# Gate products of an RG-LRU on the two row halves of the TensorE array

## The chip, the core and the metric

The kernel runs on one core of a Trainium2 chip. The metric is the device time of one execution in microseconds. A core has five engines with queues of their own: TensorE (PE, with its weight loads shown as PEld), VectorE (DVE), ScalarE (ACT), GpSimd (POOL) and SyncE (SP, which issues the DMAs here). Each engine works through its instructions in the order in which they are written, and engines wait for each other on semaphores. Matrix products are written to PSUM, eight banks of 512 float32 in each of 128 partitions; ACT and DVE read them from there.

## The reference

One layer of a hybrid decoder trunk, for a prompt of 2048 rows and for 8 decode sequences of 4 rows. After a normalised and modulated input `hn`, one projection gives six parts. Group A is an RG-LRU: a causal convolution of width 4 gives `xc`, two gates are computed from it, each with a block-diagonal matrix of 8 blocks of 64x64, and a recurrence runs along the rows:

```
r = sigmoid(einsum('blnc,ncd->blnd', xb, wa) + ba)     # xb: xc in 8 blocks of 64
i = sigmoid(einsum('blnc,ncd->blnd', xb, wx) + bx)
log_a = -8 * softplus(-lam) * r
a = exp(log_a);  u = sqrt(max(-expm1(2 * log_a), 0)) * (i * xc)
h[t] = a[t] * h[t-1] + u[t];  ya = h * silu(ga)
```

Group B (HGRN2, four heads of 128) is a chunked recurrence with decays. Both groups are joined, multiplied by an output matrix, normalised and added to the input. All inputs and outputs are float32.

## The kernel before

The prompt is worked in 8 passes (`body(n, ...)`) of 256 rows, the decode rows come after the last. Pass 0 and pass 7 are written out, passes 1 to 6 are a loop. Large products are split into three 16-bit products (`split3`, L390). The products of the recurrences, the gates and the transposes are float32; each float32 product stands in the trace as two records with a weight load each.

The order of all work is written out by hand, engine by engine. In a pass, PE runs the projections of the pass, mixed with eight levels of the HGRN2 recurrence for each half of the heads (`level`, L462 to L469), with the output product of the pass before (`out_rows`), and with the transposes of the next pass's input (`turn_x`). The channels of group A come in two halves, p = 0 and p = 1. For each half there is one call of `gates(n, p)` on PE (L507) and one of `gates_out(n, p)` on ACT (L903, L908), so there are 16 calls of each in the prompt.

The stationary of the gates, `wg`, is 128x128 for each gate and pair of blocks: two 64x64 blocks on its diagonal and zeros elsewhere, which POOL writes at the start (L1661). A call of `gates` makes four products: two of the r gate into one PSUM bank, two of the i gate into the other, each 128 rows by 128 columns by 256 moving columns. The r products raise `gr_ps`, the i products `gi_ps`. The banks are `aux[0]` and `aux[1]`, which the transposes share, so each of the two parts waits for its own bank: in the second call of a pass the r part for the copies of the transposed input (`hn_lo`), the i part for ACT's copy of the transposed keys (`kt_sb`, L865). `gates_out` then makes four sigmoids of 128x256 (two for r, two for i), and raises `r_sig` and `i_sig`.

The first call comes between level 3 and level 4 of the second half of the heads; 24 projection records follow, and then level 4, which needs DVE's scaling of that level's keys (L1166). The second call comes near the end of a pass. After it PE makes `unit(n, 1, 0)`, the rest of an output product, and `unit(n, 1, 1)`; then the next pass begins: it waits for `i_sig` of the second call, makes the 48 records of the projection `FR`, and then `turn_y` (L441), the transposes of the normalised HGRN2 rows. `turn_y` waits for `yb_ok`, that is, for the last instruction of `rows(n, 1)` on DVE (L1195).

What stands on ACT around the second call, in its order:

```
k_out(n, 1); squares_m(n - 1, 2); gates_out(n, 1); squares_o(n, 2)
squares_m(n - 1, 3); squares_o(n, 3); decay(n, 1); root(n, 1)
```

`squares_o` (L872) takes the squares of the HGRN2 rows with a sum, `squares_m` (L861) those of the output product, each activation followed by a read of the accumulator. `rows(n, 1)` on DVE begins when `squares_o(n, 3)` is done: 12 small steps for a reciprocal root, then four multiplications (L1195). After the first call ACT goes on with `xa_out(n, 1)` (L879), which waits for the 24 projection records that follow the gates, then with `decay`, `root` and the copies of the next input (`hn_out`).

In pass 0 the engines also split the weights: ACT copies pieces of the output matrix (L951), and POOL then takes the rests (L1627).

The decode rows have gates of their own: eight products with 32 moving columns (L794) and eight sigmoids (L1081).

Of the kernel before, what the change touches and what calls it, by code (L numbers as in the profile page):

```python
# [38 lines left out]
ACT = mybir.ActivationFunctionType  # L39

P = 128
# [3 lines left out]
CT = DA // P  # L45
# [14 lines left out]
DLEVELS = 2  # L60
NEWTON = 12
MAGIC = float(0x5F3759DF)

# [12 lines left out]
def build(nc, x_prompt, x_sample, state_rglru_h, state_rglru_conv, state_hgrn_S, c_prompt, c_sample, ada_w, ada_b,  # L76
          pre_norm_w, post_norm_w, w_in, conv_w, conv_b, rg_wa, rg_ba, rg_wx, rg_bx, rg_lambda, hg_lb_logits,
          hg_onorm_w, w_out, y_prompt, y_sample, h_prompt, conv_prompt, S_prompt, h_sample, conv_sample, S_sample):
    with ExitStack() as ctx:
# [33 lines left out]
        sil = sb("sil", [P, CT, T])  # L113
        wg = sb("wg", [P, 2, CT, P])

# [57 lines left out]
        u_ps = Signal("u_ps", 4)  # L173
        gr_ps, gi_ps = Signal("gr_ps", 2), Signal("gi_ps", 2)

# [116 lines left out]
        def _(sp):  # L292
# [15 lines left out]
            for i, (kind, c) in enumerate(pieces):  # L308
# [14 lines left out]
                if i == 6:  # L323
                    sp.wait_ge(zeroed, 1)
                    for w, src in ((0, rg_wa), (1, rg_wx)):
                        for odd in range(2):
                            v = src[0].rearrange("(t two) c d -> two c t d", two=2)[odd]
                            sp.dma_start(wg[64 * odd:64 * odd + 64, w, :, 64 * odd:64 * odd + 64], v).then_inc(wg_ld, 16)

# [51 lines left out]
        def _(pe):  # L381
# [50 lines left out]
            def turn_y(n, j):  # L432

                if j == 0:
                    pe.wait_ge(yb_ok.sem, yb_ok.at(n, 8))
                    pe.wait_ge(r_sig.sem, r_sig.at(n, 4))
                else:
                    pe.wait_ge(i_sig.sem, i_sig.at(n, 4))
                for h in range(2):
                    for t in range(NT):  # L440
                        last = nc.tensor.transpose(aux[j][:, T * h + P * t:T * h + P * t + P],  # L441
                                                   gbs[:, t, P * (2 * j + h):P * (2 * j + h) + P], ident[:, :])
                last.then_inc(yt_ps.sem, 1)
# [52 lines left out]
            def gates(n, p):  # L496
                pe.wait_ge(cvc.sem, cvc.at(n, 8 * p + 8))
                for w, s in ((0, gr_ps), (1, gi_ps)):
                    if p == 0 and w == 0:
                        if not isinstance(n, int) or n > 0:  # L500
                            pe.wait_ge(ytl.sem, ytl.at(n - 1, 2))
                    elif w == 1:
                        pe.wait_ge(kt_sb.sem, kt_sb.at(n, p + 1))
                    elif not (isinstance(n, int) and n == BODIES - 1):
                        pe.wait_ge(hn_lo.sem, hn_lo.at(n + 1, 2))
                    for c in range(2):
                        last = mm(aux[(1 + w + p) % 2][:, T * c:T * c + T], wg[:, w, 2 * p + c, :], xc[:, c, :],  # L507
                                  start=True, stop=True)
                    last.then_inc(s.sem, 1)

# [35 lines left out]
            def body(n, first, last_body):  # L546
# [118 lines left out]
                level(n, 1, 6)  # L665
                pe.wait_ge(r_sig.sem, r_sig.at(n, 2))
                if not last_body:
                    turn_x(n + 1, 0)
                    pe.wait_ge(i_sig.sem, i_sig.at(n, 2))
                    turn_x(n + 1, 1)  # L670
# [4 lines left out]
                else:  # L675
                    pe.wait_ge(i_sig.sem, i_sig.at(n, 2))
                    turn_decode()
# [43 lines left out]
            pe.wait_ge(wg_ld, 64)  # L721
            pe.wait_ge(zeroed, 3)
            pe.wait_ge(carry_zero, 2)
# [66 lines left out]
            pe.wait_ge(dv("conv_d"), 16)  # L790
            for w in range(2):
                for c in range(CT):
                    o = TD * CT * w + TD * c
                    last = mm(lev[1][:, o:o + TD], wg[:, w, c, :], xcd[:, TD * c:TD * c + TD], start=True, stop=True)  # L794
            last.then_inc(dv("gates_ps"), 1)
# [47 lines left out]
        def _(act):  # L843
# [54 lines left out]
            def gates_out(n, p):  # L898

                act.wait_ge(gr_ps.sem, gr_ps.at(n, p + 1))  # L900
                act.wait_ge(iu.sem, iu.at(n, p))
                for c in range(2):
                    A(rr[:, c, :], aux[(1 + p) % 2][:, T * c:T * c + T], ACT.Sigmoid,  # L903
                      bias=pcol("ba", 2 * p + c)).then_inc(r_sig.sem, 1)
                act.wait_ge(gi_ps.sem, gi_ps.at(n, p + 1))
                act.wait_ge(scan.sem, scan.at(n, 2 * p))
                for c in range(2):
                    A(ii[:, c, :], aux[p][:, T * c:T * c + T], ACT.Sigmoid, bias=pcol("bx", 2 * p + c)).then_inc(i_sig.sem, 1)  # L908

# [168 lines left out]
            for w, dst, bias in ((0, rrd, "ba"), (1, iid, "bx")):  # L1078
                for c in range(CT):
                    o = W4 * w + TD * c  # L1080
                    A(dst[:, TD * c:TD * c + TD], lev[1][:, o:o + TD], ACT.Sigmoid, bias=pcol(bias, c)).then_inc(dv("ri_d"), 1)  # L1081
            act.wait_ge(dv("ri_d"), 2 * CT)
# [28 lines left out]
        def _(dve):  # L1111
# [325 lines left out]
            rest(2)  # L1437
            dve.wait_ge(zeroed, 3)

# [132 lines left out]
        def _(pool):  # L1572
# [79 lines left out]
            def link(ins):  # L1652
# [7 lines left out]
                            base=0, channel_multiplier=1).then_inc(ident_ok, 1)  # L1660
            G.memset(wg[:, :, :, :], 0.0).then_inc(zeroed, 1)  # L1661
            pool.wait_ge(ident_ok, 1)
# [65 lines left out]
```

## Time and profile before

| what | before |
|---|---|
| median of 3 runs | 1023.69 us (1023.05 to 1025.93) |
| span of the profiled execution | 1026.3 us |
| mean granted TensorE clock | 0.981 |
| PE busy, PEld busy | 984.2 us, 714.3 us |
| DVE busy, ACT busy, POOL busy | 582.0 us, 430.0 us, 161.0 us |

The span runs from the first to the last instruction of one profiled execution, the only time that the page gives of it; it lies 2.6 us above the median of the runs and 0.4 us above the slowest of them. Busy times are sums of the records; matmuls are pipelined, so their records overlap. A granted clock of 1.0 is 2.4 GHz.

### The profile page before, as it was taken

The page shows a single profiled execution, that of the slowest core. Times are in us where ns is not written, and L with a number is a line of the kernel's source. Part 1 is how long each engine was busy: PE and PEld are TensorE (multiplying, and loading weights), DVE is VectorE, ACT ScalarE, POOL GpSimd, SP SyncE. Part 2 cuts the span into 40 slices and gives each one's busy share as a digit, 9 for nine tenths or more (in the row PEclk, how much of TensorE's full clock was granted, in tenths as well). Part 3 has the DMA queues.
Part 4 walks back from the last instruction along what each step waited for, and adds up shares of the span by engine and source line. Part 5 has one row for each costly group of instructions (what it writes and reads, how often), then busy time and mean ns, then how long its engine had stood idle before and what let it go on. Part 6 is the DMA issues. An engine that isn't in the chain of part 4 may idle for free.

```text
span 1026.3 us, 19994 instructions
## 1 busy us (share of the span) xinstructions
PE 984.2 (96%) x7423; PEld 714.3 (70%) x7478; DVE 582.0 (57%) x1652; ACT 430.0 (42%) x810; POOL 161.0 (16%) x208
## 2 busy tenths in 40 slices
PE   7899986899999999999999999999999999999987
PEld 3465875469775887579766976697759775887554
DVE  1453688436763576436754566366635773477445
ACT  2531747313651365135713373237413661345321
POOL 4000024301130112011110112011301130111212
PEclk9999998899999999999999999999999999999998
DMA  9984301100110011000110011001101010100413
GB/s 313 326 275 130 118 24 59 62 2 21 42 63 0 20 41 43 19 20 0 42 62 0 21 41 62 0 21 41 62 0 41 0 50 1 42 1 23 118 42 111
DMA packets 46590, 60.62 MB, mean 59 GB/s; under 512 B 2748, under 2 KB 40208, under 8 KB 46524
## 3 DMA queue, kind: packets, MB, share of 16 engines
q1 hardware_dynamic: 46524, 59.86, 17.8%
q8 instruction: 27, 0.44, 0.2%
q14 instruction: 39, 0.32, 0.1%
HBM read 48.90 MB, written 10.95 MB: 58 GB/s over the span
## 4 chain that ended last, share of the span: by engine, by line
PE 90%; DVE 5%; issue 2%; ACT 1%; DMA 1%; SPq 1%; DVEq 0%; ACTq 0%
PE ring L390 66%; PE lev L464 7%; PE aux L507 3%; PE okv L521 2%; PE lev L469 1%; PE okv L491 1%; PE lev L462 1%; PE ring L521 1%; PE okv L493 1%; PE okv L492 1%; DMA work<-in_w_in_dram 1%; PE okv L811 1%; PE aux L441 1%; PE aux L477 1%; PE aux L428 1%
## 5 line engine op out<-in xcount | busy, mean ns | idle before, releaser
L390 PE MATMUL ring<-hnh,wih 128*128 128x256 bf16 (+1 forms) x1152 | 291.1, 264 | 5.8 <-DVE hnl L1273 4.2
L390 PE MATMUL ring<-hnh,wil 128*128 128x256 bf16 (+1 forms) x1152 | 291.2, 264 | 0.0
L390 PE MATMUL ring<-hnl,wih 128*128 128x256 f16 (+1 forms) x1152 | 291.1, 264 | 0.0
L390 PE MATMUL ring<-woh,work 128*128 128x512 f16 x512 | 162.3, 379 | 1.7
L390 PEld LDWEIGHTS ring<-hnh,wih 128*128 128x128 f16 x1152 | 112.5, 100 | 18.1 <-issue 4.5
L1165 DVE TENSOR_TENSOR qq<-qq,gg 128x256 f32<-128x256 f32 x96 | 44.1, 459 | 140.1 <-PE lev L464 99.8
L390 PEld LDWEIGHTS ring<-hnl,wih 128*128 128x128 f16 x1152 | 110.6, 98 | 12.9
L390 PEld LDWEIGHTS ring<-hnh,wil 128*128 128x128 bf16 x1152 | 110.6, 98 | 12.4
L390 PE MATMUL ring<-wih,hnh 128*128 128x512 f16 (+1 forms) x264 | 101.1, 383 | 4.0 <-ACT kk L851 4.0
L390 PE MATMUL ring<-wih,hnl 128*128 128x512 f16 (+1 forms) x264 | 101.1, 383 | 1.4 <-issue 0.2
L1587 POOL TENSOR_TENSOR kk<-kk,cols 128x256 f32<-128x256 f32 x32 | 29.3, 935 | 419.3 <-ACT kk L851 419.3
L390 PE MATMUL ring<-wil,hnh 128*128 128x512 bf16 (+1 forms) x240 | 91.7, 382 | 0.0
L390 PEld LDWEIGHTS ring<-woh,work 128*128 128x128 bf16 (+1 forms) x512 | 50.2, 98 | 54.8
L464 PEld LDWEIGHTS lev<-qq,kk 128*128 128x128 f32 x640 | 80.9, 192 | 8.5 <-issue 2.3
L390 PE MATMUL ring<-wol,work 128*128 128x512 bf16 x225 | 85.3, 379 | 0.0
L464 PE MATMUL lev<-qq,kk 128*128 128x64 f32 x640 | 80.4, 268 | 1.8 <-DVE kk L1166 1.7
L1183 DVE SCALAR_TENSOR_TENSOR st<-st,gg,okv 128x128 f32<-128x128 f32 x64 | 19.4, 345 | 70.9 <-PE okv L493 70.9
L1173 DVE COPY_PREDICATED am<-lmask,lev 128x256 f32<-128x256 uint8 (+1 forms) x112 | 57.3, 511 | 0.0
L861 ACT ACTIVATE ring<-ring 128x512 f32<-128x512 f32 x32 | 18.6, 582 | 84.0 <-DVE work L1204 84.0
L1607 POOL TENSOR_TENSOR ii<-ii,xc 128x512 f32<-128x512 f32 x16 | 22.9, 1429 | 188.3 <-ACT ii L908 188.2
L390 PEld LDWEIGHTS ring<-wih,hnh 128*128 128x128 bf16 (+1 forms) x264 | 28.2, 107 | 29.6 <-ACT kk L851 4.3
L390 PEld LDWEIGHTS ring<-wih,hnl 128*128 128x128 f16 (+1 forms) x264 | 26.0, 99 | 31.8 <-issue 1.1
(310 smaller groups left out, 1585.5 us busy)
## 6 DMA issues: line engine op xcount, KB each, us to landing
xin<-in_x_prompt_dram SPq DMA_DIRECT2D x16, 512.0 KB, 3.4
work<-in_x_prompt_dram SPq DMA_DIRECT2D x16, 512.0 KB, 4.3
out_dram<-work SPq DMA_DIRECT2D x16, 512.0 KB, 2.6
work<-in_ada_w_dram SPq DMA_DIRECT2D x4, 1024.0 KB, 10.4
woh<-in_ada_w_dram SPq DMA_DIRECT2D x4, 1024.0 KB, 11.8
work<-in_w_in_dram SPq DMA_DIRECT2D x4, 1024.0 KB, 7.2
woh<-in_w_in_dram SPq DMA_DIRECT2D x4, 1024.0 KB, 8.5
wol<-in_w_in_dram SPq DMA_DIRECT2D x4, 1024.0 KB, 9.6
```

The costliest lines, as they stand in the source:

```text
L390: last = mm(out, a(k), b(k), start=start and k == ks[0] and j == 0, stop=stop and k == ks[-1] and j == 2)
L428: last = nc.tensor.transpose(bank[:, (k % 2) * T + P * t:(k % 2) * T + P * t + P], xin[:, t, P * k:P * k + P], ident[:, :])
L441: last = nc.tensor.transpose(aux[j][:, T * h + P * t:T * h + P * t + P], gbs[:, t, P * (2 * j + h):P * (2 * j + h) + P], ident[:, :])
L464: last = mm(lev[i % 2][:, P // 2 * hc:P // 2 * hc + P // 2], k, blocks(q, m)[:, :, 1, :], start=True, stop=True)
L507: last = mm(aux[(1 + w + p) % 2][:, T * c:T * c + T], wg[:, w, 2 * p + c, :], xc[:, c, :], start=True, stop=True)
L521: last = mm(bank[0:NS, o:o + 256], siluc[:, k, :], w[:, k, :], start=k == 0, stop=k == KT - 1)
L861: A(ring[j % 2][:, :], ring[j % 2][:, :], ACT.Square, accum_out=essq[:, j:j + 1]).then_inc(esq[j % 2].sem, 1)
L1165: V.tensor_tensor(qo, qo, g[:, :, 0:1].to_broadcast([P, nb, m]), ALU.mult).then_inc(q_upd.sem, 1)
L1173: V.copy_predicated(a[:, :, :, 1, :], msk, x).then_inc(amask.sem, 1)
L1183: V.scalar_tensor_tensor(st[:, hd, :], st[:, hd, :], gg[:, o:o + 1], okv[c][:, 2 * P + P * h:3 * P + P * h], ALU.mult, ALU.add).then_inc(s ...
L1587: G.tensor_tensor(kk[:, cols], kk[:, cols], omlb[:, hd:hd + 1].to_broadcast([P, T]), ALU.mult)\
L1607: G.tensor_tensor(ii[:, :, :], ii[:, :, :], xc[:, :, :], ALU.mult).then_inc(ix_ok.sem, 1)
```

## The change

Both gates of a pair of blocks share one stationary. `wg` shrinks from 2x4 to 4 tiles of 128x128. In rows 0 to 63 of a tile the r block stands in columns 0 to 63 and the i block in columns 64 to 127; in rows 64 to 127 it is the other way round. A product takes 64 rows of the stationary and 64 rows of `xc`, and gives r and i of one block in the two partition halves of a bank. The product of the even block goes to `aux[0]`, that of the odd block to `aux[1]`, so a call of `gates` still has four products of 256 moving columns, now of 64 rows each. All four are behind one set of waits and raise one semaphore, `g_ps`.

ACT makes each sigmoid on 64 partitions: eight instead of four for each call. The r halves lie in the partitions where they are needed; the i halves are read from one partition half and written to the other. The waits of PE on `r_sig` become waits on `i_sig`. The zero fill of `wg` on POOL goes, and with it SP's wait for it. The decode gates change in the same way: eight products of 64 rows into two banks, sixteen sigmoids.

```diff
-        wg = sb("wg", [P, 2, CT, P])
+        wg = sb("wg", [P, CT, P])
...
-                    sp.wait_ge(zeroed, 1)
                     for w, src in ((0, rg_wa), (1, rg_wx)):
                         for odd in range(2):
                             v = src[0].rearrange("(t two) c d -> two c t d", two=2)[odd]
-                            sp.dma_start(wg[64 * odd:64 * odd + 64, w, :, 64 * odd:64 * odd + 64], v).then_inc(wg_ld, 16)
+                            col = HALF * (w ^ odd)
+                            sp.dma_start(wg[HALF * odd:HALF * odd + HALF, :, col:col + HALF], v).then_inc(wg_ld, 16)
...
             def gates(n, p):
                 pe.wait_ge(cvc.sem, cvc.at(n, 8 * p + 8))
-                for w, s in ((0, gr_ps), (1, gi_ps)):
-                    if p == 0 and w == 0:
-                        if not isinstance(n, int) or n > 0:
-                            pe.wait_ge(ytl.sem, ytl.at(n - 1, 2))
-                    elif w == 1:
-                        pe.wait_ge(kt_sb.sem, kt_sb.at(n, p + 1))
-                    elif not (isinstance(n, int) and n == BODIES - 1):
-                        pe.wait_ge(hn_lo.sem, hn_lo.at(n + 1, 2))
-                    for c in range(2):
-                        last = mm(aux[(1 + w + p) % 2][:, T * c:T * c + T], wg[:, w, 2 * p + c, :], xc[:, c, :],
-                                  start=True, stop=True)
-                    last.then_inc(s.sem, 1)
+                if p == 0:
+                    if not isinstance(n, int) or n > 0:
+                        pe.wait_ge(ytl.sem, ytl.at(n - 1, 2))
+                elif not (isinstance(n, int) and n == BODIES - 1):
+                    pe.wait_ge(hn_lo.sem, hn_lo.at(n + 1, 2))
+                pe.wait_ge(kt_sb.sem, kt_sb.at(n, p + 1))
+                for c in range(2):
+                    for odd in range(2):
+                        k = slice(HALF * odd, HALF * odd + HALF)
+                        last = mm(aux[odd][:, T * c:T * c + T], wg[k, 2 * p + c, :], xc[k, c, :], start=True, stop=True)
+                last.then_inc(g_ps.sem, 1)
...
-                act.wait_ge(gr_ps.sem, gr_ps.at(n, p + 1))
+                act.wait_ge(g_ps.sem, g_ps.at(n, p + 1))
                 act.wait_ge(iu.sem, iu.at(n, p))
                 for c in range(2):
-                    A(rr[:, c, :], aux[(1 + p) % 2][:, T * c:T * c + T], ACT.Sigmoid,
-                      bias=pcol("ba", 2 * p + c)).then_inc(r_sig.sem, 1)
-                act.wait_ge(gi_ps.sem, gi_ps.at(n, p + 1))
+                    for odd in range(2):
+                        k, src = slice(HALF * odd, HALF * odd + HALF), aux[odd][:, T * c:T * c + T]
+                        ins = A(rr[k, c, :], src[k, :], ACT.Sigmoid, bias=pcol("ba", 2 * p + c)[k, :])
+                    ins.then_inc(r_sig.sem, 1)
                 act.wait_ge(scan.sem, scan.at(n, 2 * p))
                 for c in range(2):
-                    A(ii[:, c, :], aux[p][:, T * c:T * c + T], ACT.Sigmoid, bias=pcol("bx", 2 * p + c)).then_inc(i_sig.sem, 1)
+                    for odd in range(2):
+                        k, o = slice(HALF * odd, HALF * odd + HALF), slice(HALF * (1 - odd), HALF * (1 - odd) + HALF)
+                        ins = A(ii[k, c, :], aux[odd][o, T * c:T * c + T], ACT.Sigmoid, bias=pcol("bx", 2 * p + c)[k, :])
+                    ins.then_inc(i_sig.sem, 1)
...
-            G.memset(wg[:, :, :, :], 0.0).then_inc(zeroed, 1)
```

## Rows read from the trace of the kernel before

**Rows 1.** The page: busy time, share of the span and instructions of each engine.

```profile
PE 984.2 (96%) x7423; PEld 714.3 (70%) x7478; DVE 582.0 (57%) x1652; ACT 430.0 (42%) x810; POOL 161.0 (16%) x208
```

**Rows 2.** The page: shares of the chain that ended last, by engine.

```profile
PE 90%; DVE 5%; issue 2%; ACT 1%; DMA 1%; SPq 1%; DVEq 0%; ACTq 0%
```

**Rows 3.** Busy times in one pass: stretch, its length, each engine's time, granted clock.

```profile
394.40:502.80 108.40, 108.03 (x811) 80.72 (x818) 62.17 (x184) 46.63 (x92) 15.22 (x19) 1.00 0.08 29
```

**Rows 4.** Timeline of PE, pass 3, from the second gate call.

```profile
497.19 1.89 PE L507 MATMUL aux<-xc,wg 128*128 128x256 f32 x8
...
502.88 0.27 PE L390 MATMUL ring<-hnh,wih 128*128 128x256 bf16 x1
...
508.18 0.33 PE L441 MATMUL aux<-ident,gbs 128*128 128x128 f32 x1
```

**Rows 5.** Timeline of DVE, pass 3: the rows that `turn_y` waits for.

```profile
506.99 1.13 DVE L1195 SCALAR_TENSOR_TENSOR gbs<-okv,stat,gbs 128x128 f32<-128x128 f32 x4
```

**Rows 6.** Timeline of PE, pass 3, first gate call: start, duration, instructions.

```profile
473.38 1.95 PE L507 MATMUL aux<-xc,wg 128*128 128x256 f32 x8
475.16 0.27 PE L390 MATMUL ring<-hnh,wih 128*128 128x256 bf16 x1
```

**Rows 7.** Timeline of PE: products on parts of the array (rows*columns) and neighbours.

```profile
484.59 0.27 PE L390 MATMUL ring<-hnh,wil 128*128 128x256 bf16 x1
484.79 0.45 PE L469 MATMUL lev<-qq,kk 128*32 128x32 f32 x16
485.17 0.33 PE L428 MATMUL aux<-ident,xin 128*128 128x128 f32 x1
...
958.71 0.41 PE L748 MATMUL lev<-qq,kk 128*32 128x32 f32 x8
```

**Rows 8.** L469 by source: duration ns min/median/max, first and last start, forms.

```profile
L469 PE MATMUL lev<-qq,kk x384: 190/196/270, 83.3 to 923.2; 128*32 128x32 f32 x128, 128*64 128x64 f32 x64
```

**Rows 9.** Timeline of DVE, pass 3, after the first gate call.

```profile
476.20 0.42 DVE L1166 TENSOR_TENSOR kk<-kk,gg 128x256 f32<-128x256 f32 x1
```

**Rows 10.** Timeline of ACT, pass 3, around the second gate call.

```profile
496.09 0.60 ACT L865 ACTIVATE ktr<-aux 128x512 f32<-128x512 f32 x1 [2.76 <-PE aux L477]
...
499.60 0.84 ACT L903 ACTIVATE rr<-aux,par 128x256 f32<-128x256 f32 x2
500.33 0.84 ACT L908 ACTIVATE ii<-aux,par 128x256 f32<-128x256 f32 x2
501.25 0.28 ACT L872 ACTIVATE junk<-okv 128x128 bf16<-128x128 f32 x1
...
502.53 0.58 ACT L861 ACTIVATE ring<-ring 128x512 f32<-128x512 f32 x1 [0.52 <-DVE work L1204]
...
503.81 0.28 ACT L872 ACTIVATE junk<-okv 128x128 bf16<-128x128 f32 x1 [0.59 <-DVE st L1183]
```

**Rows 11.** Groups of ACT by form: count, busy us, mean ns, idle before.

```profile
L941 ACT ACTIVATE rr<-ring 9x512 f32<-9x512 f32 x1 | 0.6, 587 | 5.6 <-PE ring L521 5.6
```

**Rows 12.** Timeline of ACT, pass 3, after the first gate call.

```profile
474.50 0.84 ACT L903 ACTIVATE rr<-aux,par 128x256 f32<-128x256 f32 x2 [3.32 <-PE aux L507]
...
478.12 0.60 ACT L879 ACTIVATE xa<-ring 128x512 f32<-128x512 f32 x1 [1.92 <-PE ring L390]
```

**Rows 13.** Timeline of ACT: a square, its accumulator read, the next activation.

```profile
447.71 0.28 ACT L872 ACTIVATE junk<-okv 128x128 bf16<-128x128 f32 x1
447.88 0.19 ACT L872 ACTIVATION_READ_ACCUMULATOR junk<-okv 128x1 f32 x1
447.98 0.62 ACT L895 ACTIVATE junk<-xin 128x512 bf16<-128x512 f32 x1
```

**Rows 14.** Timeline of PE: the gate products of the decode rows.

```profile
970.34 1.97 PE L794 MATMUL lev<-xin,wg 128*128 128x32 f32 x16
```

**Rows 15.** Timelines of POOL and DVE in pass 0.

```profile
146.82 4.07 POOL L1627 TENSOR_TENSOR wol<-work,woh 128x2048 bf16<-128x2048 f32 x1
...
147.40 3.77 DVE L1165 TENSOR_TENSOR qq<-qq,gg 128x256 f32<-128x256 f32 x1 [2.25 <-PE lev L464]
```

More of the change, by code:

```diff
@@ L61 @@
 NEWTON = 12
+HALF = P // 2
 MAGIC = float(0x5F3759DF)
@@ L173, in build @@
         u_ps = Signal("u_ps", 4)
-        gr_ps, gi_ps = Signal("gr_ps", 2), Signal("gi_ps", 2)
+        g_ps = Signal("g_ps", 2)
         f_sig, k_sig, q_sb = Signal("f_sig", 2), Signal("k_sig", 2), Signal("q_sb", 2)
@@ L435, in turn_y @@
                     pe.wait_ge(yb_ok.sem, yb_ok.at(n, 8))
-                    pe.wait_ge(r_sig.sem, r_sig.at(n, 4))
-                else:
                     pe.wait_ge(i_sig.sem, i_sig.at(n, 4))
@@ L665, in body @@
                 level(n, 1, 6)
-                pe.wait_ge(r_sig.sem, r_sig.at(n, 2))
+                pe.wait_ge(i_sig.sem, i_sig.at(n, 2))
                 if not last_body:
                     turn_x(n + 1, 0)
-                    pe.wait_ge(i_sig.sem, i_sig.at(n, 2))
                     turn_x(n + 1, 1)
@@ L675, in body @@
                 else:
-                    pe.wait_ge(i_sig.sem, i_sig.at(n, 2))
                     turn_decode()
@@ L721, in _ @@
             pe.wait_ge(wg_ld, 64)
-            pe.wait_ge(zeroed, 3)
+            pe.wait_ge(zeroed, 2)
             pe.wait_ge(carry_zero, 2)
@@ L790, in _ @@
             pe.wait_ge(dv("conv_d"), 16)
[L791 to L794, printed above, removed]
+            for c in range(CT):
+                for odd in range(2):
+                    k = slice(HALF * odd, HALF * odd + HALF)
+                    last = mm((lev[1], aux[0])[odd][:, TD * c:TD * c + TD], wg[k, c, :], xcd[k, TD * c:TD * c + TD],
+                              start=True, stop=True)
             last.then_inc(dv("gates_ps"), 1)
@@ L898, in gates_out @@
             def gates_out(n, p):
-                act.wait_ge(gr_ps.sem, gr_ps.at(n, p + 1))
+                act.wait_ge(g_ps.sem, g_ps.at(n, p + 1))
                 act.wait_ge(iu.sem, iu.at(n, p))
                 for c in range(2):
-                    A(rr[:, c, :], aux[(1 + p) % 2][:, T * c:T * c + T], ACT.Sigmoid,
-                      bias=pcol("ba", 2 * p + c)).then_inc(r_sig.sem, 1)
-                act.wait_ge(gi_ps.sem, gi_ps.at(n, p + 1))
+                    for odd in range(2):
+                        k, src = slice(HALF * odd, HALF * odd + HALF), aux[odd][:, T * c:T * c + T]
+                        ins = A(rr[k, c, :], src[k, :], ACT.Sigmoid, bias=pcol("ba", 2 * p + c)[k, :])
+                    ins.then_inc(r_sig.sem, 1)
                 act.wait_ge(scan.sem, scan.at(n, 2 * p))
                 for c in range(2):
-                    A(ii[:, c, :], aux[p][:, T * c:T * c + T], ACT.Sigmoid, bias=pcol("bx", 2 * p + c)).then_inc(i_sig.sem, 1)
+                    for odd in range(2):
+                        k, o = slice(HALF * odd, HALF * odd + HALF), slice(HALF * (1 - odd), HALF * (1 - odd) + HALF)
+                        ins = A(ii[k, c, :], aux[odd][o, T * c:T * c + T], ACT.Sigmoid, bias=pcol("bx", 2 * p + c)[k, :])
+                    ins.then_inc(i_sig.sem, 1)
             def decay(n, p):
@@ L1079, in _ @@
                 for c in range(CT):
-                    o = W4 * w + TD * c
-                    A(dst[:, TD * c:TD * c + TD], lev[1][:, o:o + TD], ACT.Sigmoid, bias=pcol(bias, c)).then_inc(dv("ri_d"), 1)
+                    cols = slice(TD * c, TD * c + TD)
+                    for odd in range(2):
+                        k, o = slice(HALF * odd, HALF * odd + HALF), HALF * (odd ^ w)
+                        ins = A(dst[k, cols], (lev[1], aux[0])[odd][o:o + HALF, cols], ACT.Sigmoid, bias=pcol(bias, c)[k, :])
+                    ins.then_inc(dv("ri_d"), 1)
             act.wait_ge(dv("ri_d"), 2 * CT)
@@ L1437, in _ @@
             rest(2)
-            dve.wait_ge(zeroed, 3)
+            dve.wait_ge(zeroed, 2)
             body(0, True, False)
```

## The prediction

> **What bounds the kernel now.** I read the page's busy times first: PE is busy for 96% of the span, DVE for 57%, ACT for 42% [rows 1]. The chain of waits, second, says the same in another way: 90% of what ended last is PE's own work, 5% DVE's, 1% ACT's [rows 2]. A busy share is an average, so third I cut out one pass of the loop: in 108.40 us PE is busy for 108.03 at the full granted clock (2.4 GHz), ACT for 46.63 and DVE for 62.17 [rows 3]. So in a steady pass a microsecond less of PE work is a microsecond less of time, as long as nobody else is about to be late. Who is about to be late, I looked for in the timeline at the two gate calls, fourth, and there is one place: `turn_y` starts at 508.18, and the DVE instructions that it waits for end at 506.99 + 1.13 = 508.12 [rows 4, 5], while PE's 48 projection records before it end at about the same moment (502.88 to 508.18 is 5.30 us, 0.110 for each) [rows 4]. PE and a chain through ACT and DVE tie there. This stands alike in six passes (1 to 6); in pass 0 and pass 7 it is otherwise, and they are reckoned apart.
>
> **The products.** A call of `gates` makes eight records, and the next product starts 1.78 us after the first: 0.22 for each [rows 6]. After the change there are again eight records, each with the same 256 columns, so the same 0.22, since the step is that of the columns and not of the rows. Nothing is won unless the two halves run beside each other. No row shows two row halves, but the nearest shows two column parts. Level 6 puts 16 records of 128x32 in alternate column parts and takes 0.45 us; the decode's eight records of the same shape, all in one part, take 0.41 [rows 7]. A record lasts 0.196 [rows 8], so the steps are (0.45 - 0.20)/15 = 0.017 and (0.41 - 0.20)/7 = 0.030: two parts go at nearly twice the rate. Parts also have a price. Level 6 starts 0.20 behind the record before it, where 0.11 is usual: 0.09 to get in. It hands over at 485.17, which is 0.38 after its start, and 16 steps are 0.27: some 0.10 to get out [rows 7]. I add 0.10 for filling the second half (between 0 and one step of 0.22). A call then takes 4 x 0.22 + 0.09 + 0.10 + 0.10 = 1.17 us and saves 0.61, say 0.6 (0.49 to 0.71 by the bounds of the filling). If the halves don't overlap, it costs 0.09 + 0.10 + up to 0.10, about 0.25 more than now.
>
> The Trainium skill, "TensorE: Matmul & The Clock Gate", section "Part 3: Packing small matmuls — row/col tiling", says that products on different row groups run at once, but that matmuls are issued strictly in order. By it a call would have five slots, not four, and the kernel would come to 1020.4 us instead of 1018.6 (the first rival below). The half step of the column parts, written in the same order, speaks for four.
>
> **The first call of a pass.** PE's 0.6 counts here if what follows can come 0.6 earlier. Level 4 comes behind 24 records (2.6 us, at 477.8) and needs DVE's keys, ready at 476.62 [rows 6, 9]: 1.2 us to spare. ACT makes eight sigmoids for four. In the second call the pairs start at 499.60 and 500.33, so one costs 0.365 in a row [rows 10]; half the partitions cost the same, because an activation of 9 partitions takes 587 ns where 128 take 600 [rows 11, 12]. So ACT works 1.46 us longer. It starts at about 474.7 (0.19 later than 474.50, for getting in and filling, as it now waits for the four slots that took as long as the r part) and ends at 477.7; what it does next waited until 478.12 for PE, which would now be ready at 477.5 [rows 12]. It comes 0.2 late, and is taken up by ACT's next wait for DVE. POOL's product with `ii` starts 1.3 later, and POOL is busy for 15 of 108 us [rows 3]. So 0.6 is won in each of passes 1 to 7: 4.2 us.
>
> **The second call.** All four products now wait for the copy of the keys too; it ends at 496.69 and PE comes at 497.19 [rows 4, 10], so that wait costs nothing; were it late, the units and the next pass would queue behind it. PE's 0.6 is worth little here. ACT is the later one: it starts its sigmoids at 499.60, after a table load, long after the products. Eight end their turn at 499.60 + 8 x 0.365 = 502.52. Two squares follow (0.27 from one start to the next if the read of the sum overlaps as in [rows 13], 0.47 if not), then the square of the output product (0.59 or 0.78), and then the last squares start at 503.65 at the earliest and 504.24 at the latest. Before they started at 503.81, having waited 0.59 for DVE and before that 0.52 [rows 10]. So the two idle times of ACT just swallow the four new sigmoids. I take 503.76, near the end that the overlap shows, as the second square also waits for the first one's sum: DVE's rows and `turn_y` come 0.05 earlier, counted from the gate call (range: 0.16 earlier to 0.43 later). PE meanwhile waits for `i_sig` until 499.60 + 7 x 0.365 + 0.48 = 502.63 and again before `turn_y`. So the second call gives 6 x 0.05 = 0.3 us in passes 1 to 6. In pass 7 there is no tie behind it, only the wait for `i_sig`: by the rows of pass 3, 502.88 - 502.63 = 0.25, say 0.3.
>
> **The rest.** The decode gates make 16 records that go on for (1.97 - 0.28)/15 = 0.11 each [rows 14], three times the step of 32 columns, so their weight loads bind. If the halves load beside each other, 0.9 of 1.8 us goes, less 0.2 for getting out and filling; if not, 0.2 is lost. I take 0.6 won. The eight sigmoids more lie beside PE's output product, the last of the prompt. In pass 0 the extra 1.46 us of ACT shifts the copy of a weight piece, behind which POOL takes 4.07 us, and DVE stands still while POOL does (an instruction took 3.77 [rows 15] where one like it takes 0.42 [rows 9]). PE's 0.6 could count there, or DVE's stop could come up to 1.46 later; I take 0.3 lost. POOL's zero fill and SP's wait for it lie in the first microseconds beside the loads: nothing.
>
> **Sum.** 4.2 + 0.3 + 0.3 + 0.6 - 0.3 = 5.1 us. The span of the profiled execution becomes 1026.3 - 5.1 = 1021.2; it lies 2.6 above the median of the runs, so the median goes from 1023.69 to 1018.6. Its own range, with the bounds of filling, ACT's chain and pass 0 not all at one end, is 1016.5 to 1020.6.
>
> **The rivals.** *Strict order, five slots.* If PE takes the records as they are written (both of one product, then both of the next), only the second of a product overlaps the first of the next. A call takes 5 x 0.22 + 0.29 = 1.39 and saves 0.39; with half of the decode's gain it is 7 x 0.39 + 0.3 + 0.3 + 0.3 - 0.3 = 3.3, so 1020.4. For it: only column parts are seen to overlap fully. Against: those were written in the same order.
>
> *ACT sets the end of a pass.* If half-width sigmoids don't overlap, each costs its full 0.475 instead of 0.365, and eight take 0.88 longer. The tie at `turn_y` comes 0.88 later than in the forecast in six passes, 5.3 us: 1023.9. The decision is at the slack of ACT, 0.52 + 0.59 us before the last squares. For it: nothing is left of that slack in the forecast. Against: the four sigmoids of the trace overlap by 0.11.
>
> *The halves do not overlap*, because they share a path that the columns do not, or run as whole-array products. Then each call costs 0.25 more: 7 x 0.25 in the first calls, 6 x 0.19 in the second (0.06 of PE's slack at `turn_y`), 0.25 in pass 7, 0.2 in the decode, 0.3 in pass 0: 3.6 us slower, 1027.3. The point where it turns is a record step of (1.78 - 0.29)/8 = 0.19 us within a call: above it the kernel is slower.
>
> **How the numbers follow.** Forecast 0.50; strict order 0.17; ACT's end 0.13; no overlap 0.14; something else that makes it slower 0.06. A measurement of this kernel tells about 0.3% (3.1 us) from no change, so faster means under 1020.6, slower above 1026.8. The forecast falls under faster by nine tenths, strict order by seven, ACT's end by one: 0.45 + 0.12 + 0.01 = 0.58. Slower is 0.14 + 0.06 = 0.20, and 0.22 is left. The range 1016.5 to 1025.5 leaves out no overlap, most of what else is slower, and little below.
>
> **What would show it.** Each step: `gates` in a steady pass handing over 1.1 to 1.3 us after its start (right), 1.4 (strict order), 2.0 (no overlap); ACT's sigmoids in a row of eight, 0.36 apart; from the first product of the second call to `turn_y` 10.9 to 11.0 us, as now (10.99), with PE waiting before the next pass; a pass of 107.7 to 107.9 us for 108.4. The prediction is wrong if passes don't shorten though `gates` does, or if the gain lies in the second call.

## The result, and the profile after

The changed kernel takes 1030.26 us (median of 4 runs, 1030.09 to 1031.73) against 1024.70 us for the kernel before in the same comparison (4 runs, 1023.05 to 1025.93). The ratio is 1.0052, with a 95% interval of 1.0036 to 1.0068: slower by about half a per cent, where 1018.6 us and a gain were forecast. Timed once more beside other runs it was 1.0051 (1.0035 to 1.0067).

The profiled execution took 1031.73 us, with a span of 1030.0 us. First the busy times of the page; they answer to [rows 1]:

```profile
PE 980.2 (95%) x7478; PEld 701.5 (68%) x7478; DVE 590.3 (57%) x1652; ACT 466.2 (45%) x882; POOL 160.2 (16%) x207
```

PE is busy for 4 us less than before, and ACT for 36 us more. The chain that ended last, by engine, answers to [rows 2]:

```profile
PE 77%; DVE 11%; ACT 5%; issue 3%; DMA 1%; SPq 1%; POOL 0%; DVEq 0%; ACTq 0%; POOLq 0%
```

PE's part falls from 90% to 77%; what it loses goes to DVE and ACT. So the loss is to be looked for in waits of PE, and one pass shows them. The stretch from one pass's first projection to the next one's (columns as in [rows 3]):

```profile
397.48:506.37 108.89, 107.64 (x817) 79.10 (x817) 63.75 (x184) 50.82 (x100) 15.12 (x20) 1.00 0.08 29
```

PE is busy 107.64 us instead of 108.03, but the pass is 108.89 us long instead of 108.40: PE's busy time now falls 1.25 us short of the pass, at full granted clock. (The 0.37 before are no wait: six of that pass's 817 records are missing from the trace.) What it waits for, by the view of waits of the same execution (whole span: total us, times, longest):

```profile
PE ring L391 <- ACT ii L908: 6.8, 7, 1.0
...
PE aux L440 <- DVE gbs L1199: 1.5, 6, 0.3
```

There are two places: the next pass's first projection (L391), which waits for the i gate's sigmoids, and `turn_y` (L440), which waits for the scaled rows. The kernel before has no wait of PE at all in its steady passes. On PE's timeline the two calls of pass 3 and the two late starts answer to [rows 4] and [rows 6]:

```profile
476.84 1.13 PE L506 MATMUL aux<-xc,wg 64*128 64x256 f32 x8
477.91 0.28 PE L391 MATMUL ring<-hnh,wih 128*128 128x256 bf16 x1
...
500.04 1.14 PE L506 MATMUL aux<-xc,wg 64*128 64x256 f32 x8
501.11 0.49 PE L490 MATMUL okv<-vv,am 128*128 128x128 f32 x2
...
506.37 0.28 PE L391 MATMUL ring<-hnh,wih 128*128 128x256 bf16 x1 [1.03 <-ACT ii L908]
```

Both calls hand over 1.07 us after their start (1.78 and 1.73 before): the two row halves do run beside each other, as forecast. But the next pass begins 6.33 us after the second call instead of 5.69. ACT's timeline at the second call (it answers to [rows 10]) shows why:

```profile
501.06 1.28 ACT L902 ACT_TABLE_LOAD   x1
502.36 1.93 ACT L902 ACTIVATE rr<-aux,par 64x256 f32<-64x256 f32 x4
504.31 1.93 ACT L908 ACTIVATE ii<-aux,par 64x256 f32<-64x256 f32 x4
506.26 0.28 ACT L869 ACTIVATE junk<-okv 128x128 bf16<-128x128 f32 x1
...
507.05 0.59 ACT L858 ACTIVATE ring<-ring 128x512 f32<-128x512 f32 x1
...
507.66 0.27 ACT L869 ACTIVATE junk<-okv 128x128 bf16<-128x128 f32 x1
```

Four sigmoids of 64x256 take 1.93 us, and eight run from 502.36 to 506.24, where four of 128x256 ran from 499.60 to 501.17. One sigmoid lasts as long as before (0.469 us on the mean of the 64 of line 902, 0.470 for full width), but the next begins only 0.48 to 0.50 later, no longer 0.365. ACT's idle times of 0.52 and 0.59 before the last squares are gone, and squares follow each other without a gap; the last two start 7.62 us after the call instead of 6.62. DVE's rows answer to [rows 5]:

```profile
510.83 1.13 DVE L1199 SCALAR_TENSOR_TENSOR gbs<-okv,stat,gbs 128x128 f32<-128x128 f32 x4
```

The rows end at 511.96, 11.92 us after the second call's start; before it was 10.93. `turn_y` starts 11.97 us after the call in passes 1 to 6 (10.99 before).

Where the time is, in four stretches of the profiles (two executions of each kernel, the second ones from the experiments; "first call" is the first product of `gates` in a pass, `G0` that of pass 0 and `G7` that of pass 7):

| stretch, us | before | changed |
|---|---|---|
| start to G0 | 138.17, 136.83 | 137.61, 134.72 |
| pass 0, G0 to the next first call | 118.35, 117.35 | 121.43, 120.86 |
| passes 1 to 6, each | 108.43, 108.43 | 108.90, 108.89 |
| G7 to the end | 119.17, 119.27 | 117.55, 117.36 |

The steady passes cost 6 x 0.465 = 2.8 us, pass 0 some 3.3, and the end gives back 1.8: 4.3 us. The start scatters between 134.7 and 139.3 us over the twelve profiles of this case, with no order by kernel. It goes with stretches ahead of G0 in which the granted clock is 0.50: the profile with 134.72 has none, those with 138.17, 138.32 and 139.28 have three each. The 5.0 to 5.6 us of the timed runs fit this within that scatter.

Part of them goes with the clock. Beside the second timing of the changed kernel, the kernel before took 1025.72 us (median of 17) in runs whose mean granted clock was 0.984 to 0.986, and 1027.82 (median of 6) in those at 0.981. The changed kernel took 1028.02 in its one run at 0.984, 1029.66 and 1030.30 at 0.980 to 0.981, and 1031.41 to 1031.89 in the three at 0.976. At like clock it is slower by some 2.2 us, and the rest of the 5.0 goes with its lower clock; whether its longer waits in pass 0 lower it, no run tells.

### The profile page after: what moved, and what is told of

Its sections match the earlier page's. It is cut to its first block, busy times and chain, and to the rows that moved or that the text cites. A ratio compares the mean times of both kernels' runs of the same rounds, so it can differ in the third digit from the quotient of the medians.

```text
span 1030.0 us, 20111 instructions
## 1 busy us (share of the span) xinstructions
PE 980.2 (95%) x7478; PEld 701.5 (68%) x7478; DVE 590.3 (57%) x1652; ACT 466.2 (45%) x882; POOL 160.2 (16%) x207
## 4 chain that ended last, share of the span: by engine, by line
PE 77%; DVE 11%; ACT 5%; issue 3%; DMA 1%; SPq 1%; POOL 0%; DVEq 0%; ACTq 0%; POOLq 0%
PE ring L391 57%; PE lev L463 6%; DVE xc L1237 2%; PE okv L519 2%; PE lev L461 1%; PE lev L468 1%; PE ring L519 1%; DVE hnl L1277 1%; ACT ii L908 1%; ACT rr L902 1%; PE aux L506 1%; PE okv L490 1%; DMA work<-in_w_in_dram 1%; ACT L902 1%; PE okv L492 1%
## 5 line engine op out<-in xcount | busy, mean ns | idle before, releaser
L391 PE MATMUL ring<-hnh,wih 128*128 128x256 bf16 (+1 forms) x1152 | 291.5, 264 | 13.1 <-ACT ii L908 6.8
L391 PE MATMUL ring<-hnl,wih 128*128 128x256 f16 (+1 forms) x1152 | 291.2, 264 | 0.0
L391 PE MATMUL ring<-hnh,wil 128*128 128x256 bf16 (+1 forms) x1152 | 291.2, 264 | 0.0
L391 PE MATMUL ring<-woh,work 128*128 128x512 f16 x512 | 162.3, 379 | 0.0
L391 PEld LDWEIGHTS ring<-hnh,wih 128*128 128x128 f16 x1152 | 112.4, 100 | 28.8 <-issue 14.4
L391 PEld LDWEIGHTS ring<-hnh,wil 128*128 128x128 bf16 x1152 | 110.7, 98 | 12.5
L391 PEld LDWEIGHTS ring<-hnl,wih 128*128 128x128 f16 x1152 | 110.7, 98 | 12.2 <-issue 0.4
L391 PE MATMUL ring<-wih,hnh 128*128 128x512 f16 (+1 forms) x264 | 101.3, 384 | 3.6 <-ACT kk L848 3.6
L391 PE MATMUL ring<-wil,hnh 128*128 128x512 bf16 (+1 forms) x264 | 101.2, 384 | 0.0
L391 PE MATMUL ring<-wih,hnl 128*128 128x512 f16 (+1 forms) x264 | 101.1, 383 | 0.0
L391 PE MATMUL ring<-wol,work 128*128 128x512 bf16 x256 | 97.0, 379 | 0.0
L391 PEld LDWEIGHTS ring<-woh,work 128*128 128x128 bf16 (+1 forms) x512 | 50.0, 98 | 54.8
L975 ACT ACTIVATE gbs<-ring 128x512 f32<-128x512 f32 x16 | 9.6, 598 | 89.7 <-PE ring L391 89.7
L391 PEld LDWEIGHTS ring<-wih,hnh 128*128 128x128 bf16 (+1 forms) x264 | 28.2, 107 | 29.3 <-ACT kk L848 3.9
```

The lines of the kernel that those rows point to most:

```text
L391: last = mm(out, a(k), b(k), start=start and k == ks[0] and j == 0, stop=stop and k == ks[-1] and j == 2)
```

## The experiments

My theory: the products gain all that they were to gain, the half-width sigmoids lose more, because they don't overlap, and the loss reaches the end through PE's two waits. The rivals: the loss is on the array or in its clock; the first wait alone is the loss; ACT's length goes another way. All times are medians in us; the time before is that of the same chip.

| run | time | before | ratio, 95% interval | steady pass |
|---|---|---|---|---|
| e1_full_sigmoids | 1019.18 | 1027.03 | 0.9925 (0.9909 to 0.9941) | 107.35 |
| e2_old_products_half_sigmoids | 1035.25 | 1027.03 | 1.0081 (1.0065 to 1.0097) | 109.50 |
| e3_sigmoids_by_half | 1026.78 | 1027.03 | 0.9997 (0.9986 to 1.0008) | 108.38 |
| e4_fr_waits_r | 1029.80 | 1027.03 | 1.0029 (1.0019 to 1.0040) | 108.89 |
| a2_changed_again | 1030.86 | 1025.83 | 1.0051 (1.0035 to 1.0067) | 108.89 |
| e7_turn_y_behind_q | 1025.06 | 1025.83 | 0.9989 (0.9977 to 1.0001) | 107.95 |
| e8r_both | 1020.22 | 1025.83 | 0.9945 (0.9928 to 0.9962) | 107.31 |
| e9_first_call_only | 1023.52 | 1025.83 | 0.9981 (0.9971 to 0.9990) | 107.83 |
| e11_before_turn_y | 1025.96 | 1026.11 | 0.9993 (0.9982 to 1.0004) | 108.32 |
| b2_before_again | 1025.80 | 1026.11 | one run, for its profile | 108.43 |

**The products alone.**

```diff
-for c: for odd: A(rr[half], aux[odd][half], Sigmoid)     # 4 of 64x256, and 4 for ii
+for c: A(rr[:, c, :], aux[0][:, T*c:T*c+T], Sigmoid)     # 2 of 128x256
+for c: A(ii[:, c, :], aux[1][:, T*c:T*c+T], Sigmoid)     # 2 of 128x256
```

> The changed kernel, but ACT takes four full-width 128x256 sigmoids a call, as before, from bank 0 for the r gate and bank 1 for the i gate; it leaves out the sorting of the halves, so its values are other numbers. Theory (the eight half-width sigmoids alone cost the time, and the products on the two row halves gain what their handover shows, 1.07 us against 1.78 and 1.73): the i gate is done about 4.0 us after the start of the second call instead of 6.2, the next pass's first product waits for nothing, turn_y starts 10.3 to 11.0 us after the call, and a steady pass takes 107.1 to 107.8 us against 108.43 before and 108.90 after. Six passes, the last pass, pass 0 and the decode then give 1015 to 1020 us. Rival (the loss is on the array or in its clock, and ACT's length is hidden): the pass stays at 108.7 or more and the time at 1028 to 1031.

Measured: 107.35 a pass, ratio 0.9925. The view of waits shows none of PE between 390 and 498 us. The busy row of a stretch of one pass's length, and ACT's four sigmoids of the second call:

```profile
390.14:497.50 107.36, 106.99 (x811) 79.12 (x816) 63.03 (x184) 46.39 (x92) 15.02 (x19) 1.00 0.08 30
...
497.18 0.84 ACT L900 ACTIVATE rr<-aux,par 128x256 f32<-128x256 f32 x2
497.91 0.84 ACT L903 ACTIVATE ii<-aux,par 128x256 f32<-128x256 f32 x2
```

`turn_y` starts 10.43 us after the second call, 0.56 earlier than before. So nothing is lost on the array; the products are worth 1.08 us a pass as long as ACT stays as it was.

**The sigmoids alone.**

```diff
 # the kernel before, its eight full-height products kept
-A(rr[:, c, :], aux[(1 + p) % 2][:, T*c:T*c+T], Sigmoid)  # and ii likewise
+for odd: A(rr[half(odd), c, :], aux[(1 + p) % 2][half(odd), T*c:T*c+T], Sigmoid)
```

> The kernel before with its eight full-height products a call, but each 128x256 sigmoid cut into two 64x256 ones, so that ACT has the changed kernel's eight a call. Theory (the sigmoids alone cost the time): each takes 0.48 us in a row, the i gate ends about 6.3 us after the second call's start instead of 3.98, the last squares end about 1.1 us later, turn_y starts about 12.0 us after the call instead of 10.99, and a pass takes 109.4 to 109.6 us; six of them and 1 to 3 us more in pass 0 give 1031 to 1036 us. Rival (ACT's length is hidden): 108.43 a pass and 1024 to 1026 us.

Measured: 109.50 a pass and 1.0081; `turn_y` starts 12.05 us after the second call. PE's waits in the stretch of pass 3, and ACT's two groups of four:

```profile
PE ring L390 <- ACT ii L913: 0.6, 1, 0.6
PE aux L441 <- DVE gbs L1201: 0.2, 1, 0.2
...
502.37 1.93 ACT L905 ACTIVATE rr<-aux,par 64x256 f32<-64x256 f32 x4
504.32 1.92 ACT L913 ACTIVATE ii<-aux,par 64x256 f32<-64x256 f32 x4
```

The two waits of the changed kernel stand here without any changed product. The groups of four take 1.93 and 1.92 us, though all four of a group lie in one bank. This run and the one before add up: 108.43 + 1.07 for the sigmoids is 109.50, and the changed products under those sigmoids give 0.60 of it back (108.90), that of the first call. In the second call ACT decides, and faster products there bring `turn_y` only 0.08 us nearer to the call (11.97 for 12.05).

**The order of the sigmoids.**

```diff
-for c in range(2): for odd in range(2): A(rr[half(odd), c, :], ...)
+for odd in range(2): for c in range(2): A(rr[half(odd), c, :], ...)   # and ii likewise
```

> The changed kernel with its eight sigmoids in another order: both column groups of one partition half and bank follow each other, then both of the other half. Theory A (a sigmoid overlaps the one before it only where that read the same half and bank): every second step is 0.37 to 0.40 us instead of 0.48, a call is some 0.4 us shorter on ACT, a pass about 108.5 us, the time 1026 to 1028.5 us. Theory B (64-partition sigmoids never overlap, whichever half and bank): all steps stay at 0.48 to 0.50 and the time at 1029.5 to 1031 us.

Measured: 108.38 a pass, ratio 0.9997, the better end of theory A. ACT's timeline at the second call:

```profile
500.04 1.67 ACT L902 ACTIVATE rr<-aux,par 64x256 f32<-64x256 f32 x4
501.74 1.67 ACT L909 ACTIVATE ii<-aux,par 64x256 f32<-64x256 f32 x4
```

Four take 1.67 us, not 1.93. The first two take 0.83 together and the first three 1.31:

```profile
500.04 0.83 ACT L902 ACTIVATE rr<-aux,par 64x256 f32<-64x256 f32 x2
...
500.04 1.31 ACT L902 ACTIVATE rr<-aux,par 64x256 f32<-64x256 f32 x3
```

One sigmoid lasts 0.463 here, so the second begins 0.37 after the first and overlaps it, and the third, on the other half, begins 0.84 after the first, when the second has ended. So it is the change of partition half between one activation and the next that takes the overlap away, not the width. The bank plays no part: the run before alternated halves within one bank and had no overlap, and the full-width sigmoids of the first run go from bank 0 to bank 1 with 0.36 from start to start. This one line of order is worth 0.51 us a pass.

**The first of the two waits taken away.**

```diff
-pe.wait_ge(i_sig.sem, i_sig.at(n - 1, 4))    # ahead of the next pass's first projection
+pe.wait_ge(r_sig.sem, r_sig.at(n - 1, 4))
```

> The changed kernel, but the next pass's first projection waits for the r gate's sigmoids and no longer for the i gate's. Theory (two waits lie behind ACT, one after the other: the projection's, 1.2 us a pass, and turn_y's on the scaled rows, whose chain begins with ACT's squares behind the i gate): the first wait goes, turn_y still starts about 11.9 us after the second call and waits 1.5 us instead of 0.4, a pass stays at 108.8 to 108.95 us and the time at 1029 to 1031 us. Rival (the projection's wait alone costs the time): a pass of 107.7 us and 1021 to 1024 us.

Measured: 108.89 a pass, as without the edit. PE's waits in the stretch of pass 3 are down to one:

```profile
PE aux L440 <- DVE gbs L1199: 1.4, 1, 1.4
```

It has grown from 0.2 to 1.4, and `turn_y` starts 11.97 us after the call, as in the changed kernel. The wait that the view put first was worth nothing by itself; the one behind it was only covered by it. The ratio of 1.0029 lies below the changed kernel's, with intervals that overlap. The steady passes don't show where from; the mean granted clock of the kernel before, to which the ratio is taken, was 0.981 in 12 of its 23 runs on this chip and in 6 of 23 on that of the changed kernel's second timing.

**The changed kernel again.**

> The changed kernel once more, unaltered, so that it is timed on the chip of the runs beside it. A ratio of 1.003 to 1.007 to the kernel before, a pass of 108.90 us.

Measured: 1.0051 and 108.89.

**Both waits taken away.** 

```diff
 project(ring[0], FR, ...)                   # waits for r_sig, as above
-turn_y(n - 1, 0); turn_y(n - 1, 1)
+pe.wait_ge(usq.sem, usq.at(n - 1, 8))       # the last squares
 project(ring[1], Q_, ...)
+turn_y(n - 1, 0); turn_y(n - 1, 1)          # ACT: q_out ahead of y_turned
```

> The changed kernel with its sigmoids as they are, but the next pass's first projection waits for the r gate alone, and turn_y stands behind the Q projection instead of ahead of it (ACT copies q before the turned rows). Theory (ACT's 2.2 us more reach the end only through those two places on TensorE): the rows are scaled some 12 us after the second call's start and turn_y is now wanted at 15.6, so neither place waits, and a pass takes 107.3 to 107.5 us, as with the four full-width sigmoids (107.35); the ratio to before is 0.990 to 0.996. Rival (ACT's length also delays what follows through the next pass's gate sigmoids or VectorE's recurrence): a pass of 108.0 us or more, a ratio above 0.998.

Measured: 107.95 a pass (1 to 5), ratio 0.9989: of the 1.55 us between the changed kernel's pass and that with full-width sigmoids 0.95 come back. The pass lies between the theory and the rival; the ratio is the rival's. What is left is a third wait, further on (one pass):

```profile
PE lev L463 <- DVE qq L1156: 0.5, 1, 0.5
```

Level 0 of the next pass waits for DVE's first product. The timeline of POOL and DVE ahead of it shows the last pass's recurrence coming late: POOL copies its rows, and DVE's subtraction waits for the copy:

```profile
409.08 2.01 POOL L1587 TENSOR_TENSOR work<-sil,stat 128x1024 bf16<-128x1024 f32 x1
...
411.12 1.23 DVE L1266 TENSOR_TENSOR work<-sil,work 128x1024 f16<-128x1024 f32 x1 [0.59 <-POOL work L1587]
...
412.26 0.69 DVE L1156 TENSOR_TENSOR qq<-qq,ff 128x512 f32<-128x512 f32 x1
```

So ACT's 2.2 us reach PE by a third way, through the recurrence on DVE and POOL. My theory had only two. The link from ACT to these rows is read from the timeline; the next run bears it out.

**Order and place together: the version that beats both.** The edit is the last two taken together, with the i gate's halves in the order 1, 0.

> As the run with turn_y behind the Q projection, with the sigmoids ordered by partition halves as well, and the i gate's halves begun with the half that the r gate's last two wrote (the r gate's last read and wrote partitions 64 to 127; the i gate's first reads 0 to 63 and writes 64 to 127). Steady passes: 107.3 to 107.5 us, TensorE has no wait left there to lose; pass 0, where it waits for ACT and VectorE, 0 to 2 us shorter, so a ratio of 0.988 to 0.995. For the overlap: if the half that is written decides, the step from the r gate's last to the i gate's first is 0.37 us; if the half that is read decides, 0.48.

Measured: 1020.22, ratio 0.9945 (0.9928 to 0.9962) to the kernel before, which is 1.0% under the changed kernel on the same chip (1030.86). Passes 1 to 5 take 107.30 to 107.33 us, with PE busy throughout:

```profile
363.13:470.44 107.31, 107.31 (x817) 79.08 (x816) 63.01 (x185) 49.84 (x99) 15.05 (x19) 1.00 0.08 30
```

ACT's groups of four still take 1.67 each and begin 1.70 apart. The last two of the r gate by themselves, and POOL's copy of the rows, follow:

```profile
495.96 1.67 ACT L904 ACTIVATE rr<-aux,par 64x256 f32<-64x256 f32 x4
497.66 1.67 ACT L911 ACTIVATE ii<-aux,par 64x256 f32<-64x256 f32 x4
...
496.80 0.83 ACT L904 ACTIVATE rr<-aux,par 64x256 f32<-64x256 f32 x2
...
407.46 2.01 POOL L1589 TENSOR_TENSOR work<-sil,stat 128x1024 bf16<-128x1024 f32 x1
```

The last of the r gate read and wrote partitions 64 to 127; here the first of the i gate writes the same and reads the others, in the run ordered by halves it read the same and wrote the others. There is no overlap in either (0.48 from start to start): the half that is read and the half that is written must both stay. POOL's copy comes 44.33 us after the first gate call of its pass, where it came 44.95 after it in the run before, and the third wait is gone.

**The change in the first call alone.**

```diff
 # gates(n, 0): the changed products, sigmoids by halves
 # gates(n, 1): two block-diagonal 128x128 weights, 4 sigmoids of 128x256, as before
```

> The change in the first call of a pass alone, with its sigmoids ordered by partition halves; the second call has the eight full-height products and four full-width sigmoids of before (the decode keeps the changed products). Theory: the first call gives 0.60 us a pass, since ACT's extra time there lies beside the projections, and the second call is as before: passes of 107.8 us, a ratio of 0.994 to 0.997. Rival (ACT's extra time of the first call reaches turn_x and the next hn rows): a pass of 108.3 us or more and a ratio of 0.999 or more.

Measured: 107.83 a pass, as expected, and no wait of PE in a steady pass; but the ratio is 0.9981 (0.9971 to 0.9990), short of the expected 0.994 to 0.997. By passes 3.6 us should be won, and its profile has 2.0 more behind the first call of pass 7 (117.16 us to the end), but 2.3 are. What is missing goes with the clock: its mean was 0.977 to 0.983 in these runs, and 0.984 to 0.986 in 17 of the 23 of the kernel before. Against the six of those at 0.981 (median 1027.82) the nine at 0.980 to 0.983 (median 1023.34) gain 4.5 us, a ratio of 0.9956. In its profile the first gate call comes at 139.28 us, the latest of all twelve; this kernel loads both forms of the weights and has POOL's zero fill back. Whether these two lower its clock, no run tells.

**The control.**

```diff
 # the kernel before, with turn_y behind the Q projection and the wait for r_sig; nothing else
```

> The kernel before, with turn_y behind the Q projection and the first projection's wait on the r gate alone, as in the two runs that moved them in the changed kernel; nothing of the change itself. Theory (TensorE had no wait in a steady pass before, so there is none to take away; the gain of those runs is that of the products): 108.3 to 108.45 us a pass, a ratio of 0.998 to 1.002. Rival (moving turn_y is what gave the time): 107.9 us or less, a ratio below 0.997.

Measured: 108.32 a pass and 0.9993 (0.9982 to 1.0004), no difference. The gain of the best version needs the changed products; moving `turn_y` only keeps it.

**The kernel before again.**

> The kernel before, unaltered, for a second profile of its start and its first pass: 108.43 us a steady pass; the first gate call at 134 to 139 us and pass 0 of 117.5 to 119 us, if pass 0's 120.9 and 121.4 us in the two profiles of the changed kernel come from the change; 120 us or more if they are the scatter of that stretch.

Measured: pass 0 took 117.35 us, and 117.62 in the control, against 120.86 to 121.43 in the four profiles that have the changed products and the changed sigmoids in their first order. The 117.35 lie just under the expected range and far from the 120 of the rival. The 3.3 us of pass 0 are the change's.

## Why the prediction was wrong

**What bounds the kernel.** Right: a steady pass was PE's work, with a tie at `turn_y`. That tie is the place where the loss came in.

**The products.** Right, with four slots chosen against five. The 1.17 us worked out hold 0.09 for getting in, which falls ahead of the first record: in the first call it now starts 0.20 us behind the record before it, where it was 0.11. With the 1.07 to hand over that makes 1.16. The list of signs asked for a handover of 1.1 to 1.3 and so counted the getting in as part of it. The decode's sixteen records hand over after 1.01 us instead of 1.81, so 0.8 is won there and not 0.6. (Their 0.11 a record before is nearly four times the 0.030 of the prediction's step of 32 columns, not three; nothing hangs on it.) The two halves start together; the decode's first records show it:

```profile
975.76 0.29 PE L790 MATMUL lev<-xin,wg 64*128 64x32 f32 x1
975.77 0.29 PE L790 MATMUL aux<-xin,wg 64*128 64x32 f32 x1
975.89 0.27 PE L790 MATMUL lev<-xin,wg 64*128 64x32 f32 x1
975.90 0.27 PE L790 MATMUL aux<-xin,wg 64*128 64x32 f32 x1
```

By the strict order that the Trainium skill, "TensorE: Matmul & The Clock Gate", section "Part 3: Packing small matmuls — row/col tiling", gives, with both records of a product ahead of the next product's, a call would have needed a fifth slot (1.39 by the prediction's working); the traces show four, so that rival is out, and so is "the halves do not overlap".

**The first call.** Right: 0.61 us, from 23.81 between the two calls of a pass to 23.20, and ACT's extra time there is hidden.

**The step that failed** is that of ACT: "half the partitions cost the same [...] So ACT works 1.46 us longer", at 0.365 for one in a row. That one alone costs the same was right (0.469). That eight would follow each other as four of full width had done rests on no row: the overlap came from full-width activations, and the row of few partitions (9x512) is of one that stands alone behind idle time. The edit alternates partition halves from one sigmoid to the next, and at each such step the overlap of 0.11 is gone. (The Trainium skill, "ScalarE: Activation LUTs", section "What ACT_TABLE_LOAD costs", has activations in a row overlap by about 93 ns. The traces agree with it as long as the partitions stay, with 0.09 to 0.12 us, and only then.) From the first sigmoid to the square behind the last ACT takes 2.2 us longer (502.36 to 506.26, against 1.65 for four). The rest of the working of the second call holds with that number: the slack of 0.52 + 0.59 swallows 1.1 of it, and `turn_y` comes 0.98 later instead of 0.05 earlier. In the terms of the sum, the 0.3 us that the second call was to give in passes 1 to 6 became 6.4 lost: the first call won 6 x 0.60 there, and 2.8 are lost in all. What lies behind the first call of pass 7 gave 1.8, where 1.5 was forecast.

**The rival that came true** is "ACT sets the end of a pass". It named the lost overlap, the place and the price in a steady pass (0.88 later at the tie than in the forecast; 0.98 + 0.05 = 1.03 measured), and by it the passes would have taken 108.7 us; they take 108.90. It put the loss down to the width of the sigmoids, where the run ordered by halves shows it to be the change of half. It was given 0.13, against which the overlap of the full-width sigmoids was brought, the very thing that the edit takes away. Its sum came to 1023.9 us, next to the 1023.69 of the kernel before, because it had 1.4 us lost in the steady passes (2.8 measured) and 0.3 in pass 0, the second term that was mis-sized: 3.3 are lost there. PE's waits between 134 and 262 us, first the kernel before, then the changed one, say where:

```profile
PE ring L390 <- ACT kk L851: 4.0, 1, 4.0
PE aux L477 <- DVE kk L1166: 4.0, 1, 4.0
PE aux L507 <- DVE hnl L1273: 3.3, 1, 3.3
PE lev L469 <- DVE kk L1166: 1.7, 1, 1.7
PE okv L491 <- DVE st L1183: 0.8, 1, 0.8
```

```profile
PE aux L506 <- DVE hnl L1277: 4.4, 1, 4.4
PE aux L476 <- DVE kk L1170: 3.7, 1, 3.7
PE ring L391 <- ACT kk L848: 3.6, 1, 3.6
PE lev L468 <- DVE kk L1170: 3.5, 1, 3.5
```

The second gate call waits 4.4 us instead of 3.3, and level 6 waits 3.5 instead of 1.7 (4.3 for 3.3 and 2.7 for 1.5 in the second profiles). Pass 0 is a pass in which PE waits anyway, so each later result counts there, and while PE waits the granted clock falls to 0.50 (1.2 GHz): from 156 to 162 us PE is busy for 1.1 to 1.4 us in these four profiles. By the granted clock of the stretches from 150 to 174 us the low clock lasts some 10 us in both profiles of the kernel before, and 20 and 14 us in those of the changed one. That alone doesn't set the length of the pass: it lasts 20 us in the run ordered by halves, with a pass 0 of 119.45 us, and 14 in that of the first call alone, with 118.09. One stretch of the first profile of each, the kernel before and then the changed one (columns as in [rows 3]):

```profile
168.00:174.00 6.00, 5.21 (x48) 4.71 (x47) 3.17 (x13) 4.82 (x11) 1.83 (x1) 1.00 0.52 178
```

```profile
168.00:174.00 6.00, 5.21 (x25) 4.58 (x25) 2.30 (x5) 5.14 (x13) 1.29 (x2) 0.51 0.52 178
```

In 5.21 us of busy time PE makes 48 records in the one and 25 in the other. The loss of pass 0 isn't all ACT's length: pass 0 took 120.54 us with full-width sigmoids and the changed products, 120.52 with half-width sigmoids and the old products, 119.45 with the changed products and the sigmoids ordered by halves, and 118.09 with the change in the first call alone. What the changed products do to it isn't settled. That all four now wait for the copy of the keys together, where the r gate's two used to go ahead of it, is a candidate: with full-width sigmoids it is what the second call of pass 0 waits for.

```profile
PE aux L506 <- ACT ktr L862: 4.8, 1, 4.8
```

It was not tried by itself.

## What to carry to other kernels

When one wide instruction is cut into two narrow ones, ask not only what one costs but whether it still overlaps its neighbour, and look for a row in which the neighbours differ as they will after the edit; here, keeping activations of one partition half together was worth as much as half of what the edit gained on PE. A gain on the engine that bounds the kernel is kept only where no other engine ties with it: at a tie, work added to the other engine is paid as far as it exceeds that engine's slack. A wait that a view names first may only cover the next one, so take both away before judging either.

## What the runs showed of the hardware

- Two activations in a row overlap by about 0.1 us (0.36 to 0.38 from start to start; 64x256 sigmoids of 0.463 to 0.470 each, or 128x256 ones of 0.470 to 0.479) if both read the same partitions and both write the same; if the half read or the half written changes, the next starts 0.47 to 0.50 after. Whether the bank changes makes no difference.
- fp32 products on the two row halves of the array start 6 to 8 ns apart, pair by pair, in the steady passes and the decode. In the first call of pass 3 the pairs start at 476.84, 477.16, 477.38 and 477.60, and the next product at 477.91: steps of 0.22, with 0.10 more behind the first pair and 0.09 more behind the last. Getting in costs 0.09 (0.205 us behind the record before, 0.111 for whole-array products). All three cost what the prediction took them for.
